# Second feed-forward product of a hybrid layer: from weights standing to tokens standing

## The chip, the cores and the metric

The kernel runs on one core of a Trainium2 chip. The metric is the device time of one execution in microseconds, lower is better. TensorE's matmuls are called PE here and its weight loads PEld; VectorE is DVE, ScalarE ACT, GpSimd POOL, and SP is the engine that issues most transfers.

## The reference, cut to what matters

One layer for 128 context tokens and 512 latent tokens (640 together, 1024 channels): a token mixer, a residual with layer norm, a feed-forward block of width 2816, and a second residual with layer norm. The change is in the last three lines.

```python
x = layer_norm(ALPHA * x + g1 * out, p['ln_gain'][l, 0], p['ln_bias'][l, 0])
h2 = x * (1 + sc2) + sh2
a, u = jnp.split(h2 @ p['w_ffn_in'][l], 2, axis=-1)
f = (jax.nn.silu(a) * u) @ p['w_ffn_out'][l]          # (640, 2816) @ (2816, 1024)
x = layer_norm(ALPHA * x + g2 * f, p['ln_gain'][l, 1], p['ln_bias'][l, 1])
```

`g2` is one vector of 1024 values for the context tokens and another for the latent ones. `layer_norm` goes over the 1024 channels of a token.

## The kernel before, in words

Every large product is made of rounded fp32r parts: an operand is split into a high part and the rest (`w_hi`, `w_lo`; `f_hi`, `f_lo`), and three matmuls (high x high, high x low, low x high) are added up in PSUM. Weights come in units of 128 x 1024 floats (512 KB) by SP's queue into the two slots of `raw`; a unit is split into the two slots of `w_hi` and `w_lo`. Semaphores carry the order: `raw_in` (landed), `w_half` (high part made), `w_split` (both made), `units_done` (PE has used the unit, the slot is free). There is no planner: each engine runs its own program, written out by hand, and SP loads a unit when the one two before it has been split.

**First feed-forward product (L1379 to L1431, L1405 is its matmul).** 22 pairs of 128-channel tiles, by a scheme of seven products per pair. Its results pass through `held`, `quarter_*`, `gate_sum`, `gate_normed`, ACT's `gate`, `unit_sum` and `gated`, the last pair's steps on DVE at L2724 to L2738, and leave in `f_all` (22 tiles of 128 channels x 640 tokens, channels on the partitions). ACT rounds them to `f_hi` (L2022) and DVE makes `f_lo` (`f_rest`, L2688 to L2692, whose subtraction is recorded at L2082). The pairs of weights are loaded by `pair_load` (L712, recorded at L715); the one for the third pair goes out behind the store of the first residual's result to memory (`x1_dram`, L725).

**Second product (L1433 to L1465, matmuls at L987).** Weights stand, tokens move. For each of the 8 tiles of 128 output channels, 22 blocks of weights (three units of 8, 8 and 6 blocks), and for each block three weight parts, each against 640 tokens as a matmul of 256 and one of 384 columns: 132 matmuls a tile, 1056 in all. Two PSUM regions (`joined(0)`, `joined(1)`) take turns, and the first two tiles are interleaved (`FF_ORDER`), because `f_lo` is made while PE already runs (it waits on `f_ok` block by block). POOL makes both halves of every unit (`last_split`: `rounded` at L795, `rest` at L799).

**Residual and rows.** While PE is at the next tile, DVE normalises the stored first-residual result for it (`normed_x1`, L2747), ACT scales it (L2040), DVE adds gate times product to it (`residual`, L2541, recorded at L2546), PE transposes the result, five 128x128 blocks (`to_rows`, L1445, recorded at L1451), ACT copies the rows to `rows2` (L2048) and DVE takes statistics of the 128 columns (`row_stats`, L2757, recorded at L2762).

**End.** After the last channel tile: its residual, transposes, copy, statistics, then `bn_aggr` for the five token tiles (L2779), one square root, one reciprocal (L2797), and for each of four token tiles two 1024-column passes on DVE (`centred` L2785 and `finished` L2791) with gain and bias read from PSUM, while ACT and POOL finish the fifth (L2067, L973, L975). SP stores each token tile when it is finished (L779) and waits for all of them.

**The same form elsewhere.** One earlier product already has tokens standing and 512 weight columns moving: the mixer's `v` projection, L1295 to L1303.

Of the kernel before, what the change touches and what calls it, by code (L numbers as in the profile page):

```python
# [25 lines left out]
F32 = mybir.dt.float32  # L26
F32R = mybir.dt.float32r
# [33 lines left out]
UB = 8  # L61
UW = UB * P
FQ = (UB, UB, KF - 2 * UB)
# [11 lines left out]
U_END = U_FF2 + len(FQ) * KD  # L75
# [4 lines left out]
FF_ORDER = ((0, 0), (1, 0), (0, 1), (1, 1), (0, 2), (1, 2))  # L80
# [43 lines left out]
def build(nc, wunits, wmod1, wmod2, xT, x_fold, cT, c_rows, bmod, consts, dft_pos, dft_x, wnyq, wgate, gate_bias,  # L124
# [3 lines left out]
    with ctx:  # L128
# [8 lines left out]
        x1_dram = nc.dram_tensor("x1_dram", [P, KD, NT], F32, kind="Internal").ap()  # L137

# [216 lines left out]
        assert c2[0] <= t_end  # L355
        x2_all = at("x2_all", [P, KD, NT], F32, c2)
        rows2 = at("rows2", [P, TT, DMODEL], F32, c2)
        ln_row = at("ln_row", [P, 2, DMODEL], F32, c2)
        r2_t = at("r2_t", [P, 2, NT], F32, c2)
        stats2 = at("stats2", [P, TT, KD, 6], F32, c2)  # L360
# [132 lines left out]
        y_ok_p = sem("y_ok_p")  # L493
# [12 lines left out]
        c_read, u_read = Again(bmod_ok, 1), Again(once, 2)  # L506
        pair_in = [Again(mod_in[8], 48), Again(mod_in[9], 48)]

        ln_ps = flat[:, 0:2 * DMODEL].rearrange("p (a c) -> p a c", a=2)
# [46 lines left out]
        def by_half(ap):  # L556

            return ap.rearrange("p (h k) t -> p h k t", h=2)

# [7 lines left out]
        def _(sp):  # L567
# [157 lines left out]
            sp.dma_start(x1_dram, r_all[:]).then_inc(x1_stored, 16)  # L725

# [11 lines left out]
            def unit_load(i, n, p, q, place):  # L738

                w = FQ[q] * P  # L740
                sp.dma_start(place[:, 0:w], wunits[U_FF2 + len(FQ) * (2 * i + p) + q][:, 0:w])\
                    .then_inc(raw_in[n % 2], 16)

            def last_unit(i, n, p, q):

                sp.wait_ge(w_split, C_FF2 + 2 * len(FQ) * i + n - 1)
                unit_load(i, n, p, q, raw[:, n % 2, :])
# [9 lines left out]
            for n in range(2):  # L757
                unit_load(0, n, *FF_ORDER[n], first_raw[:, n * UW:(n + 1) * UW])
            slots_made(KF)
            for n in range(2, 4):  # L760
                sp.wait_ge(w_split, C_FF2 + n - 1)
                unit_load(0, n, *FF_ORDER[n], raw[:, n % 2, :])
# [4 lines left out]
            last_unit(0, 4, *FF_ORDER[4])  # L767
            sp.dma_start(x2_all[:, 2:KD, :], x1_dram[:, 2:KD, :]).then_inc(x_in[1], 16)
            last_unit(0, 5, *FF_ORDER[5])
            sp.wait_ge(f_f_ok, KF)  # L770
            sp.dma_start(ln_row[:], ln_rows).then_inc(table_in, 16)
            with sp.Fori(1, KD // 2) as i:
                for n in range(2 * len(FQ)):
                    last_unit(i, n, n // len(FQ), n % len(FQ))

            for tt in range(TT):
                sp.wait_ge(*((y_ok_p, 2) if tt == TT - 1 else (y_ok, tt + 1)))
                dst = y_prompt if tt == 0 else y_sample[(tt - 1) * P:tt * P, :]
                sp.dma_start(dst, rows2[:, tt, :]).then_inc(y_stored, 16)  # L779
            sp.wait_ge(y_stored, 16 * TT)  # L780
# [4 lines left out]
        def _(pool):  # L785
# [162 lines left out]
            def last_split(i, n, q, src=raw, early=False):  # L948

                slot = n % 2  # L950
                src, hi, lo = (t[:, slot, 0:FQ[q] * P] for t in (src, w_hi, w_lo))
                pool.wait_ge(raw_in[slot], 16 * len(FQ) * i + 16 * (C_FF2 // 2 + n // 2 + 1))
                if not early:
                    pool.wait_ge(units_done, C_FF2 + 2 * len(FQ) * i + n - 1)
                elif slot == 1:
                    pool.wait_ge(prod_done[P7].sem, prod_done[P7].base + KF)
                rounded(src, hi)
                pool.wait_ge(w_half, half1 + 2 * len(FQ) * i + n + 1)
                if early and slot == 1:
# [3 lines left out]
            for n in range(2):  # L963
                last_split(0, n, 0, first_raw.rearrange("p (a c) -> p a c", c=UW), True)
            for n in range(2, len(FF_ORDER)):
                last_split(0, n, FF_ORDER[n][1])
            with pool.Fori(1, KD // 2) as i:
                for n in range(2 * len(FQ)):
                    last_split(i, n, n % len(FQ))

            last = rows2[:, TT - 1, :]
            pool.wait_ge(norm_ok, 2)
            pool.tensor_tensor(last, last, ln_row[:, 0, :], ALU.mult).then_inc(y_ok_p, 1)  # L973
            pool.wait_ge(y_ok_p, 1)
            pool.tensor_tensor(last, last, ln_row[:, 1, :], ALU.add).then_inc(y_ok_p, 1)  # L975
# [3 lines left out]
        def _(pe):  # L979
# [453 lines left out]
            def last_unit(i, n, p, q, ready=None):  # L1433

                if q == 0:
                    pe.wait_ge(taken[p], A_FF2 + i + 1)
                unit_cols(joined(p), C_FF2 + 2 * len(FQ) * i + n, n % 2, f_hi, f_lo, k0=UB * q, nb=FQ[q],
                          first=(q == 0), last=(q == 2), ready=ready)

            def last_tile(i, p):  # L1440

                for q in range(len(FQ)):
                    last_unit(i, len(FQ) * p + q, p, q)

            def to_rows(i, p):  # L1445

                pe.wait_ge(taken[p], A_FF2 + i + 2)
                pe.wait_ge(rows2_ok, 2 * i + p + 1)
                for tt in range(TT):
                    a = (4 + 2 * p) * 512 + tt * P  # L1450
                    ins = pe.transpose(flat[:, a:a + P], r2_t[:, p, tt * P:(tt + 1) * P], ident)  # L1451
                ins.then_inc(rt2_done, 1)

            pe.wait_ge(c_read.sem, c_read.base + KF)
            for n, (p, q) in enumerate(FF_ORDER):
                if n == 1:
                    pe.wait_ge(u_read.sem, u_read.base + KF)
                last_unit(0, n, p, q, f_ok if p == 0 else None)
            to_rows(0, 0)
            with pe.Fori(1, KD // 2) as i:  # L1460
                last_tile(i, 0)
                to_rows(i - 1, 1)
                last_tile(i, 1)
                to_rows(i, 0)
            to_rows(KD // 2 - 1, 1)  # L1465
# [3 lines left out]
        def _(act):  # L1469
# [573 lines left out]
            def row_tile(j, p):  # L2043
# [3 lines left out]
                a = (4 + 2 * p) * 512  # L2047
                A_(dst, flat[:, a:a + NT].rearrange("p (t c) -> p t c", c=P), ACT.Copy).then_inc(rows2_ok, 1)  # L2048

            for j in range(2):  # L2050
                scaled_x1(j)
            row_tile(0, 0)
            with act.Fori(1, KD // 2) as i:
                for p in range(2):
                    scaled_x1(2 * i + p)
                row_tile(2 * i - 1, 1)
                row_tile(2 * i, 0)
            row_tile(KD - 1, 1)
            act.wait_ge(table_in, 64)
            act.wait_ge(taken[0], A_FF2 + KD // 2 + 1)  # L2060
            A_(ln_ps[:, 0, :], ln_row[:, 0, :], ACT.Copy).then_inc(sd_b_ok, 1)
            act.wait_ge(var_b_ok, 2)
            A_(sd[:], sd[:], ACT.Sqrt).then_inc(sd_b_ok, 1)
            act.wait_ge(taken[1], A_FF2 + KD // 2 + 1)
            A_(ln_ps[:, 1, :], ln_row[:, 1, :], ACT.Copy).then_inc(sd_b_ok, 1)
            act.wait_ge(norm_ok, 1)
            A_(rows2[:, TT - 1, :], rows2[:, TT - 1, :], ACT.Identity, scale=rstd[:, TT - 1:TT],  # L2067
               bias=nmr[:, 0:1]).then_inc(norm_ok, 1)
# [3 lines left out]
        def _(v):  # L2072
# [599 lines left out]
            def gated(i):  # L2672

                v.wait_ge(u_read.sem, u_read.base + i + 1)
                v.tensor_tensor(tb[:], tb[:], rstd_ps, ALU.mult).then_inc(tb_ok, 1)
# [50 lines left out]
            sum_7(KF - 1, 1)  # L2726
            f_rest(0, 1)
# [12 lines left out]
            v.wait_ge(w_split, C_FF2 + 3)  # L2740
            f_rest(*range(10, 16))
            v.wait_ge(w_split, C_FF2 + 4)
            f_rest(*range(16, KF))
            v.tensor_copy(rstd_sb[:], rstd_ps).then_inc(rstd_b_ok, 1)
            v.wait_ge(rstd_b_ok, 2)
# [8 lines left out]
            for j in range(2):  # L2754
                normed_x1(j, 0)

            def row_stats(j):  # L2757

                v.wait_ge(rows2_ok, j + 3)
                tiles = rows2[:, :, :].rearrange("p t (j c) -> p t j c", c=P)  # L2760
                for tt in range(TT):
                    ins = v.bn_stats(stats2[:, tt, j, :], tiles[:, tt, j, :])  # L2762
                return ins
# [5 lines left out]
            with v.Fori(1, KD // 2) as i:  # L2769
                for p in range(2):  # L2770
                    normed_x1(2 * i + p, 1)
# [168 lines left out]
```

## Time and profile before

| | |
|---|---|
| median of 3 runs | 1405.27 us (1404.27 to 1405.46) |
| the profiled execution's own time | 1404.05 us |
| its span on the core | 1402.2 us |
| granted TensorE clock, mean | 0.993 of full speed |
| PE / DVE / POOL / ACT busy | 98% / 61% / 57% / 32% of the span |

The profile is one execution; busy time is summed over the span, and PE's matmuls are pipelined, so two of them overlap in the records and only the distance between starts is their real pace. "The chain that ended last" goes back from the last instruction, at each step to what released it. In a row of a timeline the bracket says how long the engine had idled before and what released it.

### The profile page before, as it was taken

What the parts mean: (1) busy time and instruction counts of PE and PEld (TensorE: products, weight loads), DVE (VectorE), ACT (ScalarE), POOL (GpSimd) and SP (SyncE); (2) the same over time, 40 slices, a digit from 0 to 9 for tenths busy, and PEclk for the clock granted to TensorE, in tenths of its full rate; (3) what the DMA queues carried; (4) which work ended last, traced back from release to release, by engine and by line L of the source; (5) the groups of instructions that cost most, each with busy time, mean ns of one, the idle gap of its engine ahead of it and who ended that gap; (6) DMA issues with size and microseconds to landing.
All of it is one profiled execution on the core that took longest, in us unless ns stands there. A gap on an engine that the chain in (4) does not pass through costs nothing. (4 is left out here: it accounts for less than half of the span.)

```text
span 1402.2 us, 24166 instructions
## 1 busy us (share of the span) xinstructions
PE 1369.4 (98%) x9089; PEld 1327.0 (95%) x9089; DVE 862.2 (61%) x1473; ACT 450.3 (32%) x806; POOL 795.5 (57%) x444
## 2 busy tenths in 40 slices
PE   9999999999999999999999999999999999999994
PEld 5999999899999989999999999999999999999994
DVE  6975983357436624752674577587777777892224
ACT  4824221231222122122233100466555445600001
POOL 0264865632552363245235666458998888865662
PEclk9999999999999999999999999999999999999997
DMA  9634633221411321142146454422222221242221
GB/s 379 220 115 139 226 121 132 85 65 50 141 63 68 105 91 60 49 143 74 37 140 230 168 202 156 172 89 109 89 89 90 90 88 63 92 154 84 67 67 75
DMA packets 57483, 164.01 MB, mean 117 GB/s; under 512 B 6072, under 2 KB 20544, under 8 KB 56264
## 3 DMA queue, kind: packets, MB, share of 16 engines
q1 hardware_dynamic: 38712, 142.48, 29.2%
q10 hardware_dynamic: 18704, 20.68, 4.4%
q8 instruction: 36, 0.59, 0.2%
q14 instruction: 31, 0.25, 0.1%
HBM read 145.81 MB, written 17.33 MB: 116 GB/s over the span
## 5 line engine op out<-in xcount | busy, mean ns | idle before, releaser
L795 POOL TENSOR_TENSOR w_hi<-raw,zero 128x1024 fp32r<-128x1024 f32 (+1 forms) x101 | 192.2, 1903 | 436.4 <-PE psum L987 358.6
L799 POOL TENSOR_TENSOR w_lo<-raw,w_hi 128x1024 fp32r<-128x1024 f32 (+2 forms) x116 | 278.7, 2402 | 29.3 <-ACT w_hi L1881 16.9
L1405 PE MATMUL psum<-t_r,ws_r 128*128 128x322 f32 x1848 | 276.6, 311 | 2.0 <-POOL ws_r L871 0.7
L1405 PEld LDWEIGHTS psum<-t_r,ws_r 128*128 128x128 f32 x1848 | 275.1, 189 | 3.2 <-issue 2.0
L987 PE MATMUL psum<-h_hi,w_hi 128*128 128x256 f32 (+1 forms) x768 | 176.4, 311 | 0.3 <-PEq L1341 0.3
L987 PE MATMUL psum<-h_lo,w_hi 128*128 128x256 f32 (+1 forms) x768 | 175.3, 309 | 0.0
L987 PE MATMUL psum<-h_hi,w_lo 128*128 128x256 f32 (+1 forms) x768 | 175.1, 309 | 0.0
L871 POOL TENSOR_TENSOR ws_r<-ws_f,ws_r 128x512 fp32r<-128x512 f32 x88 | 124.4, 1414 | 33.6 <-DVE ws_f L2619 20.8
L987 PEld LDWEIGHTS psum<-h_lo,w_hi 128*128 128x128 f32 x768 | 140.3, 189 | 0.0
L987 PEld LDWEIGHTS psum<-h_hi,w_lo 128*128 128x128 f32 x768 | 140.0, 188 | 0.0
L987 PEld LDWEIGHTS psum<-h_hi,w_hi 128*128 128x128 f32 x768 | 138.7, 189 | 1.4 <-issue 0.7
L871 POOL TENSOR_TENSOR ws_r<-pair,ws_r 128x512 fp32r<-128x512 f32 x66 | 95.7, 1450 | 4.6 <-ACT ws_r L1939 4.6
L987 PE MATMUL psum<-f_hi,w_hi 128*128 128x256 f32 x352 | 81.2, 312 | 1.8 <-DVE f_lo L2082 1.7
L987 PE MATMUL psum<-f_lo,w_hi 128*128 128x256 f32 x352 | 80.1, 309 | 0.0
L987 PE MATMUL psum<-f_hi,w_lo 128*128 128x256 f32 x352 | 80.1, 309 | 0.0
L1939 ACT ACTIVATE ws_r<-ws_f 128x512 fp32r<-128x512 f32 x88 | 54.3, 630 | 71.1 <-POOL ws_f L890 36.8
L987 PEld LDWEIGHTS psum<-f_hi,w_hi 128*128 128x128 f32 x352 | 63.4, 188 | 2.8 <-DVE f_lo L2082 2.5
L2546 DVE SCALAR_TENSOR_TENSOR r_t<-psum,mod_sb,x_all 128x128 f32<-128x128 f32 (+1 forms) x16 | 8.1, 546 | 93.5 <-PE psum L987 93.5
L987 PEld LDWEIGHTS psum<-f_lo,w_hi 128*128 128x128 f32 x352 | 64.1, 188 | 0.0
L987 PEld LDWEIGHTS psum<-f_hi,w_lo 128*128 128x128 f32 x352 | 64.0, 188 | 0.0
L1301 PE MATMUL psum<-w_hi,h_hi 128*128 128x512 f32 x160 | 62.3, 390 | 0.0
L1301 PE MATMUL psum<-w_lo,h_hi 128*128 128x512 f32 x160 | 62.3, 389 | 0.0
(353 smaller groups left out, 3121.9 us busy)
## 6 DMA issues: line engine op xcount, KB each, us to landing
raw<-in_wunits SPq DMA_DIRECT2D x118, 512.0 KB, 3.3
pair<-in_wunits SPq DMA_DIRECT2D x46, 512.0 KB, 4.2
mod_slot<-in_wmod SPq DMA_DIRECT2D x16, 512.0 KB, 14.6
mod_ring<-in_wmod ACTq DMA_DIRECT2D x16, 512.0 KB, 3.4
yg_dram<-yg_sb ACTq DMA_DIRECT2D x20, 256.0 KB, 2.5
yg_st<-yg_dram SPq DMA_DIRECT2D x16, 320.0 KB, 3.6
c_raw<-in_stateC SPq DMA_DIRECT2D x4, 1028.0 KB, 6.2
z_ring<-in_wmod SPq DMA_DIRECT2D x8, 512.0 KB, 4.5
```

Of the source, the lines that this page charges most:

```text
L795: pool.tensor_tensor(hi, src, zero[:, 0:1].broadcast_to([P, src.shape[1]]), ALU.add)\
L799: pool.tensor_tensor(lo, src, hi.bitcast(F32), ALU.subtract).then_inc(w_split, 1)
L871: pool.tensor_tensor(ws_r[n][:, 1, :], src, ws_r[n][:, 0, :].bitcast(F32), ALU.subtract)\
L987: ins = mm(out[:, a:z], w[:, slot, cols], x[:, k, a:z], start=(start and n == 0), stop=(stop and n == 2))
L1301: ins = mm(psum[:, v_banks[tt], :], x[:, k, tt * P:(tt + 1) * P], w[:, q % 2, cols], start=(k == 0 and n == 0), stop=(k == KD - 1 and n == 2))
L1405: ins = mm(out, ws_r[n][:, w, cols], t_r[:, n, k, x, :], start=(starts and k == 0 and m == 0), stop=(k == HALF_K - 1 and m == 2), skip_gro ...
L1939: A_(ws_r[n][:, 0, :], src, ACT.Copy).then_inc(ws_hi_ok[n].sem, 1)
L2546: ins = v.scalar_tensor_tensor(out=out[:, span], in0=src[:, span], scalar=mod_sb[:, gcol + j, g:g + 1], in1=r[:, j, span], op0=ALU.mult, o ...
```

## The change

The second product is turned round. A unit of weights is now two blocks of 128 feed-forward channels (`KU`) times 512 output channels (`UC`); there are 11 units (`NU`) for the left half of the output channels and 11 for the right. A block of `f_hi` or `f_lo` for 128 tokens stands and 512 weight columns move, into one PSUM bank for each token tile: five banks a half (`ROW_BANKS`). So PE issues 2 halves x 11 units x 5 token tiles x 2 blocks x 3 parts = 660 matmuls of 512 columns. In the right half the last four units are kept together (the extra places `last_hi`, `last_lo` hold their parts in memory that has come free) and are run token tile by token tile.

```diff
+            def row_part(h, tt, u, first, last):
+
+                out, toks = psum[:, ROW_BANKS[h][tt], :], slice(tt * P, (tt + 1) * P)
+                hi, lo = unit_slot(u)
+                for n in range(KU):
+                    k, cols = KU * (u % NU) + n, slice(n * UC, (n + 1) * UC)
+                    if h == 0 and tt == 0:
+                        pe.wait_ge(f_ok, k + 2)
+                    for m, (f, w) in enumerate(((f_hi, hi), (f_hi, lo), (f_lo, hi))):
+                        ins = mm(out, f[:, k, toks], w[:, cols], start=(first and n == 0 and m == 0),
+                                 stop=(last and n == KU - 1 and m == 2))
+                return ins
...
+            BANK_FREE = ((u_read.sem, u_read.base + KF - 1), (c_read.sem, c_read.base + KF),
+                         (c_read.sem, c_read.base + KF), (ta_ok, KF), (u_read.sem, u_read.base + KF))
+            for u in range(NU):
+                pe.wait_ge(w_split, C_FF2 + SPLITS.index(u) + 1)
...
+                if 2 <= u < KD + 2:
+                    x1_to_rows(u - 2)
+            pe.wait_ge(rows2_ok, KD + 2)
+            for u in range(NU, FIRST_LAST):
...
+                    if u == NU and tt >= 3:
+                        pe.wait_ge(row_sum_ok, tt - 2)
...
+            for tt in range(TT):
+                for u in range(FIRST_LAST, 2 * NU):
...
+                ins.then_inc(tile_done, 1)
```

The first-residual result alone (not the sum) is transposed, tile by tile between the left half's units 2 to 9 (`x1_to_rows`); ACT copies it to `rows2`. When a half of a token tile is complete, DVE multiplies the bank by `g2` and adds it to `rows2` (`row_sum`). `g2` must for this lie along the columns: SP writes it from `mod_sb` (channels on partitions) to memory in two transfers, right behind the store of the first-residual result and ahead of the third pair's weights, and reads it back to all partitions later.

```diff
             sp.dma_start(x1_dram, r_all[:]).then_inc(x1_stored, 16)
+            sp.wait_ge(mod_sum1, 5 * KD)
+            for g in range(2):
+                sp.dma_start(g2_dram[g].rearrange("k p -> p k"), mod_sb[:, 5 * KD:6 * KD, g],
+                             allow_slow_non_contiguous=True).then_inc(g2_stored.sem, 16)
...
+            sp.dma_start(g2_row[:], g2_dram.rearrange("g k p -> g (k p)").unsqueeze(0).broadcast_to([P, 2, DMODEL]))\
+                .then_inc(g2_in.sem, 16)
```

From the third unit on, ACT makes the high part (`unit_hi`) and POOL only the rest. On DVE the last pair's `unit_sum` and `gated` move ahead of most of `f_rest`, and the copy of the first norm's reciprocal from PSUM (L2744) moves ahead of all of it; `normed_x1` and two `f_rest` each then alternate, held back by `w_split`.

```diff
             sum_7(KF - 1, 1)
+            v.tensor_copy(rstd_sb[:], rstd_ps).then_inc(rstd_b_ok, 1)
+            v.wait_ge(rstd_b_ok, 2)
             f_rest(0, 1)
...
-            f_rest(*range(3, 7))
+            f_rest(3)
             unit_sum(KF - 1, 1)
-            f_rest(7)
-            gated(KF - 1)
-            f_rest(8, 9)
...
+            gated(KF - 1, rstd_sb[:])
+            f_rest(4, 5)
...
+            for j in range(KD):
+                v.wait_ge(w_split, C_FF2 + j + 3)
+                normed_x1(j, 0 if j < 2 else 1)
+                f_rest(2 * j + 6, 2 * j + 7)
...
+            def row_sum(h, tt):
+
+                n, ps, g = TT * h + tt, psum[:, ROW_BANKS[h][tt], :], min(tt, 1)
+                cols = slice(h * UC, (h + 1) * UC)
+                v.wait_ge(tile_done, n + 1)
+                v.tensor_tensor(ps, ps, g2_row[:, g, cols], ALU.mult).then_inc(scaled_ok.sem, 1)
+                v.wait_ge(scaled_ok.sem, scaled_ok.base + n + 1)
+                v.tensor_tensor(rows2[:, tt, cols], ps, rows2[:, tt, cols], ALU.add).then_inc(row_sum_ok, 1)
+                v.wait_ge(row_sum_ok, n + 1)
+                return v.bn_stats(stats2[:, tt, h, :], rows2[:, tt, cols])
...
             for tt in range(TT):
+                row_sum(0, tt)
+            for tt in range(TT):
+                own(row_sum(1, tt))
+                own(v.bn_aggr(mv[:, tt, :], stats2[:, tt, :, :]))
+                v.tensor_scalar(sd[:, tt:tt + 1], mv[:, tt, 1:2], EPS, None, ALU.add).then_inc(var_b_ok, 1)
...
+                parts = [slice(0, DMODEL)] if tt < TT - 1 else [slice(0, UC), slice(UC, DMODEL)]
+                for n, cols in enumerate(parts):
+                    centred(tt, cols, tt + n)
+                v.wait_ge(sd_b_ok, tt + 2)
+                own(v.reciprocal(rstd[:, tt:tt + 1], sd[:, tt:tt + 1]))
+                for n, cols in enumerate(parts):
+                    finished(tt, cols, tt + n)
```

ACT takes the square root of one token tile at a time; gain and bias are read from `ln_row` in SBUF; all five token tiles are finished by DVE, and the last one is finished and stored in two halves of its columns. The host lays the weights of `w_ffn_out` out in the new units.

## Rows read from the trace of the kernel before

**Rows 1.** the page: span, and busy time by engine

```profile
span 1402.2 us, 24166 instructions
...
PE 1369.4 (98%) x9089; PEld 1327.0 (95%) x9089; DVE 862.2 (61%) x1473; ACT 450.3 (32%) x806; POOL 795.5 (57%) x444
```

**Rows 2.** chain that ended last, from 1215 us: start, us, what

```profile
1282.92 0.55 PE psum L1451 x5
...
1363.18 19.39 PE psum L987 x132
```

**Rows 3.** timeline of PE, 1215 to 1262 us: start, us, engine, line, out<-in

```profile
1221.49 0.56 PE L987 MATMUL psum<-f_hi,w_hi 128*128 128x256 f32 x2
...
1243.37 0.56 PE L987 MATMUL psum<-f_hi,w_hi 128*128 128x256 f32 x2 [0.96 <-DVE f_lo L2082]
```

**Rows 4.** timeline of PE, 246 to 260 us, tokens standing: first and last of 58 matmuls

```profile
246.68 0.39 PE L1301 MATMUL psum<-w_hi,h_hi 128*128 128x512 f32 x1
...
259.62 0.39 PE L1301 MATMUL psum<-w_hi,h_hi 128*128 128x512 f32 x1
```

**Rows 5.** timeline of DVE, 1205 to 1290 us

```profile
1222.21 4.70 DVE L2082 TENSOR_TENSOR f_lo<-f_all,f_hi 128x640 fp32r<-128x640 f32 x4
...
1227.02 1.13 DVE L2668 SCALAR_TENSOR_TENSOR tb<-nmu,w,psum 128x128 f32<-128x128 f32 x3
```

**Rows 6.** weight halves: POOL's timeline, then the instructions of L1881

```profile
1279.70 2.39 POOL L799 TENSOR_TENSOR w_lo<-raw,w_hi 128x1024 fp32r<-128x1024 f32 x1
...
L1881 ACT ACTIVATE w_hi<-raw x6: 1041/1046/1062, 890.6 to 927.8; 128x1024 fp32r<-128x1024 f32 x6
```

**Rows 7.** a 128x512 sum on DVE, timeline

```profile
1040.68 0.69 DVE L2619 TENSOR_TENSOR ws_f<-ws_f,pair 128x512 f32<-128x512 f32 x1
```

**Rows 8.** timeline of all engines, 1382 to 1402.2 us

```profile
1382.72 1.01 DVE L2546 SCALAR_TENSOR_TENSOR r_t<-psum,mod_sb,x_all 128x128 f32<-128x128 f32 x2 [17.44 <-PE psum L987]
...
1384.12 2.27 DVE L2762 BATCH_NORM_STATS2 stats<-rows  x10 [0.39 <-ACT rows L2048]
...
1386.43 1.29 DVE L2779 BATCH_NORM_AGGREGATE mv<-stats 128x2 f32<-128x48 f32 x5
...
1387.83 1.27 DVE L2785 SCALAR_TENSOR_TENSOR rows<-rows,mv,psum 128x1024 f32<-128x1024 f32 x1
...
1389.02 0.18 DVE L2797 RECIPROCAL rstd<-sd 128x5 f32<-128x5 f32 x1
...
1394.19 4.40 SPq L779 DMA_DIRECT2D out_y_sample<-rows  x4
...
1395.27 2.47 DVE L2791 SCALAR_TENSOR_TENSOR rows<-rows,rstd,psum 128x1024 f32<-128x1024 f32 x2
```

**Rows 9.** waits of SP's queue: total us, times, longest

```profile
SPq L128 <- DMA out_y_sample<-rows: 3.2, 1, 3.2
```

**Rows 10.** SP's timeline; a window: DMA share and GB/s; DMA issues (page)

```profile
952.38 51.48 SPq L715 DMA_DIRECT2D pair<-in_wunits  x10
...
950.00:951.00 1.00, 1.00 0.34 143
...
pair<-in_wunits SPq DMA_DIRECT2D x46, 512.0 KB, 4.2
```

**Rows 11.** timelines of ACT and POOL, then the chain, around 960 us

```profile
960.67 0.62 ACT L1939 ACTIVATE ws_r<-pair 128x512 fp32r<-128x512 f32 x1
...
965.40 1.29 POOL L871 TENSOR_TENSOR ws_r<-ws_f,ws_r 128x512 fp32r<-128x512 f32 x1
...
958.68 258.48 PE psum L1405 x1736
```

**Rows 12.** queues: of the whole span (page), then 39 to 46 us: packets, MB, share

```profile
q10 hardware_dynamic: 18704, 20.68, 4.4%
...
DMA packets 967, 2.62 MB, mean 374 GB/s; under 512 B 558, under 2 KB 558, under 8 KB 965
...
q1 hardware_dynamic: 965, 2.60, 101.3%
```

More of the change, by code:

```diff
@@ L756, in _ @@
             slots_made(KF - 1)
-            for n in range(2):
-                unit_load(0, n, *FF_ORDER[n], first_raw[:, n * UW:(n + 1) * UW])
+            for m in range(2):
+                unit_load(m, first_raw[:, m * UW:(m + 1) * UW])
             slots_made(KF)
-            for n in range(2, 4):
-                sp.wait_ge(w_split, C_FF2 + n - 1)
-                unit_load(0, n, *FF_ORDER[n], raw[:, n % 2, :])
+            unit_load(2)
             sp.wait_ge(prod_done[P4].sem, prod_done[P4].base + KF)
@@ L946, in _ @@
             half1 = half0 + U_FF1 - U_HEAD
[L948 to L959, printed above, removed]
+            for m in range(2 * NU):
+                src = first_raw[:, m * UW:(m + 1) * UW] if m < 2 else raw[:, m % 2, :]
+                hi, lo = unit_slot(SPLITS[m])
+                if m < 2:
+                    pool.wait_ge(raw_in[m], 16 * (C_FF2 // 2 + 1))
+                    if m == 1:
+                        pool.wait_ge(prod_done[P7].sem, prod_done[P7].base + KF)
+                    rounded(src, hi)
+                pool.wait_ge(w_half, half1 + m + 1)
+                if m == 1:
                     pool.wait_ge(prod_done[P4].sem, prod_done[P4].base + KF)
                 rest(src, hi, lo)
[L963 to L975, printed above, removed]
         @block.tensor
@@ L1431, in _ @@
             product(P4, KF - 1, 1)
[L1433 to L1448, printed above, removed]
+            def row_part(h, tt, u, first, last):
[9 more added lines that the diff above has]
+                return ins
@@ new lines, in _ @@
+            pe.wait_ge(rows2_ok, KD + 2)
+            for u in range(NU, FIRST_LAST):
+                pe.wait_ge(w_split, C_FF2 + SPLITS.index(u) + 1)
+                for tt in range(TT):
+                    if u == NU and tt >= 3:
+                        pe.wait_ge(row_sum_ok, tt - 2)
+                    ins = row_part(1, tt, u, u == NU, False)
+                ins.then_inc(units_done, 1)
+            for tt in range(TT):
+                for u in range(FIRST_LAST, 2 * NU):
+                    if tt == 0:
+                        pe.wait_ge(w_split, C_FF2 + SPLITS.index(u) + 1)
+                    ins = row_part(1, tt, u, False, u == 2 * NU - 1)
+                ins.then_inc(tile_done, 1)
@@ L2041, in scaled_x1, with row_tile @@
                    bias=ln_cols[:, j, 1:2]).then_inc(x1_ok, 1)
[L2043 removed]
+            def row_tile(j):
                 act.wait_ge(rt2_done, j + 1)
                 dst = rows2[:, :, :].rearrange("p t (j c) -> p t j c", c=P)[:, :, j, :]
[L2047 to L2052 removed]
@@ L2053, in _ @@
[L2053 to L2068, printed above, removed]
+                A_(dst, strip(1).rearrange("p (t c) -> p t c", c=P), ACT.Copy).then_inc(rows2_ok, 1)
+            def unit_hi(m):
+                u = SPLITS[m]
+                act.wait_ge(raw_in[m % 2], 16 * (C_FF2 // 2 + m // 2 + 1))
+                if m == 2:
+                    act.wait_ge(w_split, C_FF2 + 2)
+                if u == FIRST_LAST:
+                    act.wait_ge(rt2_done, KD)
+                elif FIRST_LAST < u < 2 * NU - 1:
+                    act.wait_ge(units_done, C_FF2 + NU + 1)
+                elif u == 2 * NU - 1:
+                    act.wait_ge(units_done, C_FF2 + FIRST_LAST - 2)
+                elif u == NU + 1:
+                    act.wait_ge(tile_done, TT)
+                else:
+                    act.wait_ge(units_done, C_FF2 + u - 1 - (u > NU + 1))
+                A_(unit_slot(u)[0], raw[:, m % 2, :], ACT.Copy).then_inc(w_half, 1)
@@ L2071, in _ @@
+            for m in range(2, 4):
+                unit_hi(m)
+            for j in range(KD):
+                scaled_x1(j)
+                unit_hi(4 + j)
+                row_tile(j)
+            for m in range(KD + 4, 2 * NU):
+                unit_hi(m)
+            for tt in range(TT):
+                act.wait_ge(var_b_ok, tt + 2)
+                A_(sd[:, tt:tt + 1], sd[:, tt:tt + 1], ACT.Sqrt).then_inc(sd_b_ok, 1)
         @block.vector
@@ L2752, in normed_x1 @@
                 v.tensor_tensor(x2_all[:, j, :], x2_all[:, j, :], rstd_sb[:], ALU.mult).then_inc(t2_ok, 1)
[L2754 to L2763, printed above, removed]
-            for p in range(2):
-                v.wait_ge(x1_ok, p + 1)
-                residual(p, p, C_FF2 + FF_ORDER.index((p, len(FQ) - 1)) + 1, x2_all, 5 * KD, r2_t[:, p, :])
@@ L2768, in _ @@
-            row_stats(0)
-            with v.Fori(1, KD // 2) as i:
-                for p in range(2):
-                    normed_x1(2 * i + p, 1)
-                v.wait_ge(x1_ok, 2 * i + 2)
-                for p in range(2):
-                    v.wait_ge(rt2_done, 2 * i + p - 1)
-                    residual(2 * i + p, p, C_FF2 + 2 * len(FQ) * i + len(FQ) * (p + 1), x2_all, 5 * KD, r2_t[:, p, :])
-                    row_stats(2 * i + p - 1)
-            own(row_stats(KD - 1))
-            for tt in range(TT):
-                ins = v.bn_aggr(mv[:, tt, :], stats2[:, tt, :, :])
@@ L2794, in _ @@
-            v.wait_ge(sd_b_ok, 2)
-            centred(0)
-            v.wait_ge(sd_b_ok, 3)
-            own(v.reciprocal(rstd[:], sd[:]))
-            v.scalar_tensor_tensor(out=nmr[:, 0:1], in0=mv[:, TT - 1, 0:1], scalar=-1.0, in1=rstd[:, TT - 1:TT],
-                                   op0=ALU.mult, op1=ALU.mult).then_inc(norm_ok, 1)
-            centred(1)
-            v.wait_ge(sd_b_ok, 4)
-            finished(0)
-            for tt in range(2, TT - 1):
-                centred(tt)
-                finished(tt - 1)
```

137 lines of the change are left out of this document (78 added, 59 removed).

## The prediction, made blind

> **What bounds the kernel now.** I read the page first: PE is busy 98% of a span of 1402.2 us [rows 1]. Then the chain of waits from 1215 us on: it is PE's own matmuls, channel tile after channel tile, 132 matmuls of the second product in 19.39 us and then five transposes in 0.55 us [rows 2]. No other engine holds PE up there, so what counts is PE's pace in that stage, its few stalls at the start, and everything that comes after its last matmul. The stage runs from 1221.49 [rows 3] to 1363.18 + 19.39 = 1382.57 [rows 2], 161.1 us; after it come 19.6 us of epilogue in which PE does next to nothing. The change works on both.
>
> **Pace of PE.** Before: 132 matmuls are 66 pairs of 256 and 384 columns, so 19.39/66 = 0.2938 us per 640 columns. Eight tiles are 155.1 us. After: 660 matmuls of 512 columns. The kernel already has this very form, tokens standing and 512 weight columns moving; its 58 matmuls start from 246.68 to 259.62, 12.94/57 = 0.2270 us apart [rows 4]. 660 x 0.2270 = 149.8 us. The columns are the same (337,920); what goes is a cost per matmul, about 13 ns, 396 times. Gain 5.3 us.
>
> The Trainium skill, in TensorE: Matmul & The Clock Gate, section Back-to-back issue gap, gives the warm distance of two lone matmuls as columns/2.4 + 2.5 ns. By that rule a pair would take 271.7 ns and a 512 matmul 215.8, and the turn would bring 1.0 us, not 5.3. Both of this trace's distances are longer, the shorter form by more.
>
> **Stalls and transposes.** 8 x 19.39 + 7 x 0.55 = 159.0, so 161.1 holds 2.1 us of stalls: PE waits for `f_lo` three times, the longest 0.96 us before 1243.37 [rows 3]. They come from the first tile needing 22 blocks of `f_lo` in about 22 us. After, the first unit needs two blocks and keeps PE for 30 x 0.227 = 6.8 us, so 22 blocks are spread over 75 us; those stalls go. All eight transposes now lie within the stage (before, the eighth was in the epilogue): 8 x 0.55 = 4.4 us.
>
> What could be late next? **Banks:** the fifth token tile of the first unit wants the bank that `unit_sum` reads, at 1221.49 + 4 x 1.36 = 1226.9. That step is at 1227.02 now, behind four `f_rest` of 4.70/4 = 1.18 us from 1222.21 [rows 5]. With one `f_rest` ahead of it, it is over by 1222.2 + 1.2 + 1.3 = 1224.7: 2 us to spare. The moved copy of the reciprocal adds about 0.8 us to DVE earlier; nothing but these steps stands behind it, and twice it would still fit. **Weights:** a unit's slot comes free when the unit two before it is done; ACT's high part takes 1.05 us, POOL's rest 2.39 [rows 6], together 3.5 us of the 6.8 that PE spends on the unit between. Loads fit in the same way. **`f_rest`:** each step of DVE's loop is two of them and two 640-column passes, some 4 us, twice a unit ahead. The turned order thus costs PE nothing; the cover is 3 us everywhere, and if it went, each unit would cost what is missing.
>
> PE's last matmul then ends at 1221.49 + 149.8 + 4.4 + 0.16 (its record is 0.39 long, its distance 0.23 [rows 4]) = 1375.9, 6.7 us earlier.
>
> **Epilogue.** Before: 1382.57 to 1402.2, of which DVE's passes over all rows last until 1395.27 + 2.47 = 1397.74 [rows 8]. After, each token tile ends 24 x 0.227 = 5.45 us behind the one before it, and DVE deals with four of them under PE. Per tile, from rows: product and sum in PSUM, 512 columns each, 0.69 [rows 7] plus 0.04 for the semaphore, so 1.46; statistics of 512 columns: no row, at least the 0.2 us of a 128-column one, at most another 512-column pass; I take 0.69, since the columns set the time of the other passes; aggregate 1.29/5 = 0.26; root's input 0.08; the two 1024-column passes 1.19 each (1387.83 to 1389.02); reciprocal 0.22 [rows 8]. Sum 5.1 us, under 5.45: no queue builds up. ACT's root lies under the first pass. For the last tile, in halves: 0.15 to start (1382.57 to 1382.72), 1.46, 0.69, 0.26, 0.08, 1.22, 0.22, 1.30 = 5.4 us. Then the stores: before, DVE's end to the span's end is 4.46 us, of which the last of four queued stores is issued until 1394.19 + 4.40 = 1398.59 [rows 8] and SP waits 3.2 us for it [rows 9]. After, the last half row is issued at once: 0.1 + 0.35 + 3.2 + 0.4 = 4.05. The smaller store may land sooner or, with rows of 2 KB, later: -0.7 to +0.7.
>
> New end: 1375.9 + 5.4 + 4.05 = 1385.3 against 1402.2: **16.9 us**, 6.7 from PE's stage and 10.2 from the epilogue. The profiled execution took 1404.05, which gives 1387.2; the median of the runs lies 1.2 above that execution, so I say **1388.4**.
>
> **The new transfers of `g2`.** They are the one thing that the trace does not price: 2 x 1024 values of 4 bytes, each with an address of its own, 128 for each of 16 DMA engines, behind the store that ends near 951 (the window from 950 still shows 0.34) and ahead of the third pair's weights, issued at 952.38 and landed 4.2 us later [rows 10]. Nearest rows: queue q10 over the span, 0.044 x 1402.2 x 16/18704 = 53 ns a packet; q1 from 39 to 46 us, where 558 of 967 packets are under 512 bytes: 1.013 x 7 x 16/965 = 118 ns a packet [rows 12]. So 128 packets are 6.8 to 15 us, and the weights land at 951 + 6.8 + 4.2 = 962.0 to 970.2. Who waits? ACT uses them at 960.67, and POOL's rest for P1 of the third pair is in order ahead of the one for P7 of the second, which starts at 965.40 [rows 11]. Counting back from 1221.49 at 258.48/1736 = 0.149 us a matmul [rows 11], 1692 matmuls, P1 starts at 969.5 and that P7 at 967.7; its slot is ready at 966.7, so there is 1 us to spare, and the weights may land until about 964.5. I take 53 ns (such packets carry next to nothing, and the second row's carry 2.7 KB on average): no cost. At 118 ns PE stalls 5.7 us. Reading `g2` and `ln_row` back is 1 MB each in a stage with DMA mostly idle: nothing.
>
> **Rivals.**
> - *Forecast holds:* 0.70.
> - *The small packets are dear, but not very (73 to 205 ns):* PE stalls 5.7 us at 118 ns, so 1394.1. For it: no row has such writes to memory. Against: loads of small packets pass among others at 118 ns at most. 0.11.
> - *Slower than before:* the same mechanism from 205 ns a packet on, where 128 packets take 26.2 us, the landing moves to 981.4 and PE's stall to 16.9 us; at 300 ns the stall is 29 us and the time 1417. 0.04. The Trainium skill, in DMA: Bandwidth & Descriptors, says under Rules for kernel authors that a strided last dimension becomes a descriptor per element, and under Specifications that below 512 bytes there is read-modify-write; it gives no price, and no row here shows one.
> - *DVE falls behind:* the tiles are then not normalised as they end. If a tile takes over 5.45 us (it would need 0.35 more, for example by passes on SBUF operands at the 1.27 us record rather than the 1.19 distance, and slower statistics), four excesses add up: at 6.4 us a tile, 4 us, so 1392. 0.05.
> - *PE waits in the new order* (a split or a bank late at the start or where the halves meet): 3 to 5 us, 1392. Against: 3 us of cover each time. 0.06.
> - *Nothing is saved per matmul:* the new form keeps the old one's time per column here, 0.2938 x 512/640 = 0.2350 us, and only stalls and epilogue gain: 1393.7. Against it stands the pace of [rows 4]. 0.04. By the rule of the Trainium skill cited above it would be 1392.7.
>
> **How the numbers follow.** Forecast's own spread is about -2.5 to +2 (statistics, last store, stalls that hide others). To hold 8 in 10 the range reaches to the sizes of the milder rivals: 1385.5 to 1394. A difference of 0.2%, 2.8 us, is about what a measurement of this kernel can tell from none. All cases but the dear packets are faster by far more: faster 0.94; around 200 ns a packet, same 0.02; beyond, slower 0.04.
>
> **What would show it.** Right: 660 matmuls 0.227 us apart from 1221.5 on, and no PE idle over 0.3 us until about 1376; the five last tile groups 5.45 us apart, DVE idle some 0.3 us between them; DVE's last pass 5.4 us behind the last matmul, the span's end 4 us on. The third pair's weights landed before 964.5 and the first product still ending at 1221.5. Wrong: ACT, DVE or POOL waiting for `pair` near 960 and PE idle near 968 (packets); `w_split` or DVE's `f_lo` releasing PE within the stage; DVE without idle time at the end and its last pass more than 7 us behind PE; 512-column matmuls at another distance than 0.227.

## The result, and the profile after

The changed kernel takes 1388.8 us in the median of 4 runs (1387.98 to 1391.49) against 1405.4 us before; the ratio is 0.9888, with a 95% interval from 0.9877 to 0.9900. The forecast was 1388.4. The profiled execution took 1387.98 us, its span is 1385.9.

The page's first rows, answering to [rows 1]:

```profile
span 1385.9 us, 23137 instructions
...
PE 1361.4 (98%) x8693; PEld 1293.3 (93%) x8693; DVE 854.0 (62%) x1458; ACT 466.1 (34%) x827; POOL 748.6 (54%) x418
```

The chain of waits of the changed kernel, from 940 and from 1215 us on (start, us, what), answering to [rows 2]:

```profile
951.53 12.99 DMA pair<-in_wunits
...
1223.70 20.45 PE psum L1455 x90
1244.14 0.55 PE psum L1465 x5
1244.69 6.86 PE psum L1455 x30
...
1296.39 81.63 PE psum L1455 x360
```

The last four rows are the new second product: 90 matmuls in 20.45 us and 360 in 81.63 are 0.227 us each, with no stall between, and the transposes are the same 0.55 us as before. The stage runs from its first matmul at 1223.54 to DVE's start on the last tile at 1378.04, 154.5 us, where it was 161.1. The first row is not of that stage. The chain of before has no transfer near that place; here it waits 13 us for the third pair's weights.

The timeline of DVE in the epilogue, the fourth token tile and the last one, answering to [rows 8]:

```profile
1372.61 0.70 DVE L2800 TENSOR_TENSOR psum<-psum,g_row 128x512 f32<-128x512 f32 x1 [0.27 <-PE psum L1455]
1373.34 0.69 DVE L2802 TENSOR_TENSOR rows<-psum,rows 128x512 f32<-128x512 f32 x1
1374.06 0.69 DVE L2804 BATCH_NORM_STATS2 stats<-rows 128x6 f32<-128x512 f32 x1
1374.79 0.21 DVE L2823 BATCH_NORM_AGGREGATE mv<-stats 128x2 f32<-128x12 f32 x1
...
1376.49 1.28 DVE L2814 SCALAR_TENSOR_TENSOR rows<-rows,rstd,ln_row 128x1024 f32<-128x1024 f32 x1
1378.04 0.70 DVE L2800 TENSOR_TENSOR psum<-psum,g_row 128x512 f32<-128x512 f32 x1 [0.27 <-PE psum L1455]
...
1382.06 1.42 DVE L2814 SCALAR_TENSOR_TENSOR rows<-rows,rstd,ln_row 128x512 f32<-128x512 f32 x2
```

Read the brackets: DVE idles 0.27 us before each of these two tiles, so it is ready when PE is, and each tile takes it 1378.04 - 0.27 - 1372.61 = 5.16 us out of PE's 5.43. The last one takes 1383.48 - 1378.04 = 5.44. The stores then end sooner than before, by SP's waits (total us, times, longest), answering to [rows 9]:

```profile
SPq L134 <- DMA out_y_sample<-rows: 1.6, 1, 1.6
```

From DVE's end to the span's end it is 2.4 us; it was 4.46. The whole epilogue is 7.9 us, it was 19.6.

What was lost is at the start of the first feed-forward product. The timeline of PE there, and the two rows of ACT's that release it:

```profile
957.74 6.71 PE L1418 MATMUL psum<-t_r,ws_r 128*128 128x322 f32 x44
965.55 2.05 PE L1418 MATMUL psum<-t_r,ws_r 128*128 128x322 f32 x12 [1.10 <-ACT held L1981]
969.76 6.49 PE L1418 MATMUL psum<-t_r,ws_r 128*128 128x322 f32 x41 [2.16 <-ACT held L1981]
...
964.54 0.63 ACT L1971 ACTIVATE ws_r<-pair 128x512 fp32r<-128x512 f32 x1 [5.36 <-DMA pair<-in_wunits]
...
969.29 0.42 ACT L1981 ACTIVATE held<-psum 128x322 f32<-128x322 f32 x1
```

ACT used the third pair at 960.67 without waiting [rows 11]; now it idles 5.36 us for it, and PE waits 3.3 us for `held`, which stands behind on ACT.

The balance of the two profiled executions: PE's stage -6.6 us, epilogue -11.7, and from the first product's first matmul to the second product's first +3.6 (280.6 to 284.2 us). The stages ahead, which the change does not touch, were 1.6 us shorter in this execution; over the traces of this study the first product starts anywhere between 939.1 and 942.3 us, so that part is drift. Together that is -16.3, the difference of the spans.

### The profile page after: what moved, and what is told of

It is laid out like the page before. It is cut to its first block and busy times, and to the rows that moved or that the text cites. A ratio compares the mean times of both kernels' runs of the same rounds, so it can differ in the third digit from the quotient of the medians.

```text
span 1385.9 us, 23137 instructions
## 1 busy us (share of the span) xinstructions
PE 1361.4 (98%) x8693; PEld 1293.3 (93%) x8693; DVE 854.0 (62%) x1458; ACT 466.1 (34%) x827; POOL 748.6 (54%) x418
## 5 line engine op out<-in xcount | busy, mean ns | idle before, releaser
L824 POOL TENSOR_TENSOR w_hi<-raw,zero 128x1024 fp32r<-128x1024 f32 x79 | 152.2, 1926 | 376.4 <-PE psum L1000 298.1
L828 POOL TENSOR_TENSOR w_lo<-raw,w_hi 128x1024 fp32r<-128x1024 f32 (+1 forms) x111 | 269.8, 2431 | 101.1 <-ACT w_hi L2097 73.5
L1455 PE MATMUL psum<-w_hi,f_hi 128*128 128x512 f32 x190 | 74.7, 393 | 0.0
L1455 PE MATMUL psum<-w_hi,f_lo 128*128 128x512 f32 x190 | 74.1, 390 | 0.0
L1455 PE MATMUL psum<-w_lo,f_hi 128*128 128x512 f32 x190 | 73.9, 389 | 0.0
L1314 PE MATMUL psum<-w_hi,h_lo 128*128 128x512 f32 x160 | 62.2, 389 | 0.0
L1000 PE MATMUL psum<-yh,w_hi 128*128 128x256 f32 (+1 forms) x256 | 58.6, 311 | 0.0
L1000 PE MATMUL psum<-yh,w_lo 128*128 128x256 f32 (+1 forms) x256 | 58.3, 308 | 0.0
L1000 PE MATMUL psum<-yl,w_hi 128*128 128x256 f32 (+1 forms) x256 | 58.1, 308 | 0.0
```

The lines of the kernel that those rows point to most:

```text
L824: pool.tensor_tensor(hi, src, zero[:, 0:1].broadcast_to([P, src.shape[1]]), ALU.add)\
L828: pool.tensor_tensor(lo, src, hi.bitcast(F32), ALU.subtract).then_inc(w_split, 1)
L1000: ins = mm(out[:, a:z], w[:, slot, cols], x[:, k, a:z], start=(start and n == 0), stop=(stop and n == 2))
L1314: ins = mm(psum[:, v_banks[tt], :], x[:, k, tt * P:(tt + 1) * P], w[:, q % 2, cols], start=(k == 0 and n == 0), stop=(k == KD - 1 and n == 2))
L1455: ins = mm(out, f[:, k, toks], w[:, cols], start=(first and n == 0 and m == 0), stop=(last and n == KU - 1 and m == 2))
```

## The experiments

The runs form three groups, each on one chip, and each kernel is compared with the kernel before on its chip. The first group holds the changed kernel, the stores moved, the stores doubled and the 256-column matmuls; the second holds the stores on ACT's queue and the two runs with fewer units kept; the third holds the rest. The second group has no run of the changed kernel, so what it says is read from its traces more than from its times. For the start of the first product one length is used: from its first matmul (940.91 in the kernel before) to the second product's first matmul (1221.49).

**The changed kernel twice more**, as the base of the first and of the third group.

> The changed kernel once more, as the base that the other runs of this call are set against. Expected by all theories: 1388 to 1391 us, the second product's PE stage 154.3 us long, about 2 us of PE waits for ACT's held rows early in the first feed-forward product.

Measured: 1393.4 us (1392.5 to 1394.9), ratio 0.9930, interval 0.9914 to 0.9947. That is 4.6 us above the first result, above what was expected here and near the upper edge of the prediction's range (1394).

> The changed kernel a third time, with more rounds, for the interval: 1388 to 1394.

Measured: 1389.1 us (1388.0 to 1390.0), ratio 0.9887 (0.9871 to 0.9904). The second product's stage and the epilogue are the same in all three, 154.5 and 7.9 us. The length at the start is not: 284.2, 286.9 and 284.8 us, where it was 280.6 before. The windows of PE show part of why (busy us and instructions, granted clock, DMA share, GB/s); first the execution of the result, then the one of 1393 us:

```profile
965.00:970.00 5.00, 2.29 (x13) 1.00 0.00 0
970.00:975.00 5.00, 5.00 (x34) 1.00 0.60 205
```

```profile
965.00:970.00 5.00, 2.65 (x18) 1.00 0.45 171
970.00:975.00 5.00, 3.71 (x16) 0.54 0.00 0
975.00:980.00 5.00, 5.00 (x28) 0.78 0.61 210
```

PE sits idle for 3.3 us in the one and 3.6 in the other, but in the second its granted clock then falls to the lower of its two levels for some microseconds, for (0.46 + 0.22) x 5 = 3.4 us at full speed. Part of that falls into the time in which PE idles anyway: the start is 6.3 us longer than before, so 6.3 - 3.6 = 2.7 us are lost beside the idle time. In the first execution the clock stays at 1.00.

**The stores of `g2` moved behind the last pair.**

```diff
             sp.dma_start(x1_dram, r_all[:]).then_inc(x1_stored, 16)
-            sp.wait_ge(mod_sum1, 5 * KD)
-            for g in range(2):
-                sp.dma_start(g2_dram[g].rearrange("k p -> p k"), ...
...
             for i in range(2, KF):
                 pair_next(i, i % 2)
+            sp.wait_ge(mod_sum1, 5 * KD)
+            for g in range(2):
+                sp.dma_start(g2_dram[g].rearrange("k p -> p k"), ...
```

> The two stores of g2 go out behind the last pair of weights instead of ahead of the third. Theory A (the 4-byte packets delay the third pair, and PE pays): PE's waits at the start of the first product go, the third pair lands some 4 us after its issue, the time falls by 3.6 us against the changed kernel, to about 1385.2. Theory B (the late start of the second product is another execution's drift and not the packets): no change, 1388 to 1389. If the packets were as harmful in the new place, the first two units of the second product would land late (after 1214) and the time would not fall.

> The version with the stores behind the last pair again, with more rounds: 1385 to 1387, 3.6 to 7 us below the changed kernel.

Measured: 1386.1 us (1384.6 to 1387.1) beside 1393.4, and 1385.8 us (1384.1 to 1388.8) beside 1389.1; ratios to the kernel before 0.9876 (0.9860 to 0.9893) and 0.9869 (0.9850 to 0.9888). That is 7.3 and 3.3 us less than the changed kernel of the same group, where 3.6 and 3.6 to 7 were expected. The length at the start is 280.3 us both times, PE has no wait for `held`, the clock stays at 1.00, and ACT uses the third pair, issued at 952.62, without waiting:

```profile
960.91 0.62 ACT L1971 ACTIVATE ws_r<-pair 128x512 fp32r<-128x512 f32 x1
```

Theory A holds, B falls. The two units loaded behind the stores in the new place land in time: POOL rounds the first at 1215.48 without waiting for it (1214.73 in the kernel before). They are issued from 1203.10 on, 11.6 us behind the stores, so this run does not show that the stores are harmless there to a load issued at once. This version is the fastest of the study, though in the third group its interval overlaps the changed kernel's.

**The stores made twice.**

```diff
             for g in range(2):
                 sp.dma_start(g2_dram[g].rearrange("k p -> p k"), mod_sb[:, 5 * KD:6 * KD, g],
                              allow_slow_non_contiguous=True).then_inc(g2_stored.sem, 16)
+            for g in range(2):
+                sp.dma_start(g2_dram2[g].rearrange("k p -> p k"), mod_sb[:, 5 * KD:6 * KD, g],
+                             allow_slow_non_contiguous=True).then_inc(g2_stored.sem, 16)
```

> The two stores of g2 are made twice in the same place, the second time to another place in memory, 4096 packets in all. Theory A, with the packets at the 80 ns each per DMA engine that the trace of the changed kernel suggests (about 10 us for 2048): the third pair lands 10 us later than in the changed kernel, all of it stalls PE, 1399 us. Theory A with a fixed cost for a DMA rather than one for a packet: the same here, since the DMAs double too. Theory B: 1389. If what counts is not the ring's order, PE stalls by much less than 10 us.

Measured: 1398.7 us (1398.0 to 1400.4), ratio 0.9966. The length at the start is 295.1 us, 14.8 more than without stores in this place; ACT idles 16.20 us for the pair:

```profile
947.80 7.83 SPq L754 DMA_DIRECT2D g_dram<-mod_sb  x2
956.22 5.60 SPq L738 DMA_DIRECT2D pair<-in_wunits  x2
...
976.97 0.63 ACT L1975 ACTIVATE ws_r<-pair 128x512 fp32r<-128x512 f32 x1 [16.20 <-DMA pair<-in_wunits]
```

So the cost grows about as A has it: the length at the start is 8 to 11 us above that of the three executions with two stores. PE idles 12.6 us of it, and the clock is at its lower level from 971 to 981. Part of it is new: SP itself was held up, and issued the pair at 956.2 instead of about 952.5.

**One store instead of two** (the context tokens' gate is left out and the latent tokens' used for both).

```diff
-            for g in range(2):
+            for g in range(1, 2):
                 sp.dma_start(g2_dram[g].rearrange("k p -> p k"), mod_sb[:, 5 * KD:6 * KD, g],
```

> Only the latent tokens' g2 is stored, 1024 packets instead of 2048, and read back for the context tokens too (their gate is left out). Theory G (the time goes with the packets, some 80 to 100 ns each per DMA engine, 10 to 12 us for 2048): the third pair lands 5 to 6 us earlier than in the changed kernel and PE's waits for ACT's held rows go: as fast as with the late stores, 1385 to 1387. Rival H (a fixed completion time of about 10 us for writes of this kind): the pair lands as late as in the changed kernel, and the 3.6 to 6.3 us of stall stay.

Measured: 1389.1 us (1387.6 to 1389.9), the time of the changed kernel in the same group. The length at the start is 284.6 us. The pair is used 12.4 us after its issue at 951.21; with both stores it was 12.5 to 14.7:

```profile
963.65 0.64 ACT L1971 ACTIVATE ws_r<-pair 128x512 fp32r<-128x512 f32 x1 [4.38 <-DMA pair<-in_wunits]
```

Theory G falls: half the packets, nearly the same delay. Rival H is nearer for one store against two, but alone it does not explain the four of the run before. How the cost depends on the count of packets and of transfers, and whether it lies in the single elements written to memory or in how they are gathered, stays open: no run stored the same values in longer pieces.

**The stores from ACT's queue.** The same lines, moved ahead of ACT's wait for the column sums.

> The two stores of g2 go out from ACT's queue, ahead of its wait for the column sums, at about the same moment as in the changed kernel. Theory E (the weights waited for their turn behind the packets in one ring): the third pair lands within 5 us of its issue, PE loses at most what ACT's own delay costs (2 x 1.4 us of issue, of which about 1.5 us were idle), 1385 to 1387. Theory F (the packets keep the DMA engines or memory busy whichever ring they are in): the pair lands as late as in the changed kernel, 1389 or more.

Measured: 1391.4 us (1388.6 to 1393.1), ratio 0.9912 (0.9895 to 0.9930). The pair is issued at 950.59 and used at 965.14, 14.5 us later, though its ring held no packet of the stores. The length at the start is 285.0 us. Theory E falls and F holds: it is not the order in the ring. The windows of that execution (granted clock, DMA share, GB/s) show hardly any data on the way:

```profile
951.00:952.00 1.00, 1.00 0.00 0
952.00:953.00 1.00, 1.00 0.00 0
953.00:954.00 1.00, 1.00 0.00 0
...
959.00:960.00 1.00, 1.00 0.20 20
...
962.00:963.00 1.00, 1.00 1.01 328
```

The DMA engines are silent for three microseconds, trickle at some 30 GB/s for eight, and only then move the pair at over 300. In this run the stores have a queue of their own, so their packets can be counted apart (packets, MB, share of 16 engines, 948 to 966 us):

```profile
q10 hardware_dynamic: 2080, 0.01, 5.3%
```

That is 0.053 x 18 x 16/2080 = 7 ns a packet, and all of them have gone by 951. Their own time is thus even less than the prediction took; what costs is the silence and the trickle behind them. In the result's execution the two stores land 16.1 and 17.5 us after their issue, near 959 and 960, just before the pair's data comes at full rate; which of the two causes the other these rows do not show.

**ACT's order in the second pair's cycle.**

```diff
                 hold(0, i, par)
-                slot_hi(P1, i + 1, 1 - par)
+                if not pending:
+                    slot_hi(P1, i + 1, 1 - par)
                 hold(1, i, par)
                 slot_hi(P7, i, par)
+                if pending:
+                    slot_hi(P1, i + 1, 1 - par)
```

> Stores of g2 in their place, but in ACT's first cycle the high part of the third pair's P1 comes behind hold(1) and P7's high part instead of ahead of them. Theory J (PE waits because hold(1) stands behind the late pair on ACT, which the prediction's deadline of 964.5 left out): PE's wait for held rows goes (3.3 to 3.6 us); what remains is POOL's rest for P7, which still stands behind P1's, up to 3 us when the pair lands at 968. Time 0.5 to 3 us below the changed kernel's of the same call. Rival: no change, since POOL's order alone sets the stall.

Measured: 1388.4 us (1387.8 to 1389.9) beside 1389.1: nothing that can be told from no change. One of PE's two waits for `held` is gone, the other is 2.45 us. Theory J named the right engine and the wrong one of its instructions. The length at the start is 284.6 us. The chain of waits of this run:

```profile
964.41 0.70 DVE ws_f L2656
...
965.79 1.28 ACT L1988
...
967.46 0.61 ACT psum L1989
968.06 0.55 ACT ws_r L1971
968.62 0.33 ACT held L1981
...
968.99 6.13 PE psum L1418 x29
```

DVE's sum for P5 needs the late pair, ACT's high part needs the sum, and behind it on ACT stand a table load of 1.28 us (its row bears the gate's line), the first gate, P4's high part, and then `hold(2)`, for which PE waits. POOL, on which the prediction had its deadline, is not on this chain.

**Two matmuls of 256 columns for each of 512.**

```diff
-                        ins = mm(out, f[:, k, toks], w[:, cols], start=(first and n == 0 and m == 0),
-                                 stop=(last and n == KU - 1 and m == 2))
+                        for a in range(0, UC, UC // 2):
+                            b = slice(a, a + UC // 2)
+                            ins = mm(out[:, b], f[:, k, toks], w[:, cols][:, b],
+                                     start=(first and n == 0 and m == 0 and a == 0),
+                                     stop=(last and n == KU - 1 and m == 2), skip_group_check=True)
```

> Each 512-column matmul of the second product is cut into two of 256, with the same block standing: 1320 matmuls. Theory C (a cost of 13 to 14 ns per matmul, whatever its columns): the pair takes 0.2407 us instead of 0.2270, the stage grows by 9.0 us to 163.3, 1397.8 us in all. By the rule of columns/2.4 + 2.5 ns for each: growth 1.6 us, 1390.4. If the cost hangs on the change of the standing block rather than on the matmul: 1388.8, no growth.

Measured: 1400.8 us (1397.4 to 1403.4), beside 1393.4 for the base; the start costs more in this execution too (287.4 us), so the stage is what counts. It runs from 1229.74 to DVE's start at 1392.59, 162.8 us instead of 154.5: 8.35 us for 660 matmuls more, 12.7 ns each. The chain of waits of this run ends with

```profile
1349.96 42.61 PE psum L1457 x355
...
1392.59 0.71 DVE psum L2803
```

which is 0.120 us a matmul. Theory C holds nearly at its size; the other two fall. The weight loads grew with the matmuls, though (9353 of each, where it was 8693): the same block is loaded again for the second half. So a cost for each matmul cannot be told here from a cost for each load.

**Fewer units kept for the last tiles.** `N_LAST` is the count of units run token tile by token tile at the end.

```diff
-N_LAST = 4
+N_LAST = 1
...
-SPLITS = (*range(NU + 2), FIRST_LAST, NU + 2, ...
+SPLITS = tuple(range(2 * NU))
```

> Only the right half's very last unit is run with its tiles ending one by one (6 matmuls, 1.36 us apart) instead of the last four (24 matmuls, 5.45 us apart). Theory D (DVE's 5.17 us a tile, measured in the changed kernel, sets the epilogue where PE is faster): DVE starts 5.45 us ahead of PE's end and needs 4 x 5.17 + 5.4 + 0.1, the epilogue grows from 7.9 to about 23 us, the time by 15.2 us to 1404. Rival: the gain of the epilogue comes from the shorter DVE work and the missing transposes, not from the overlap: growth under 5 us.

Measured: 1405.4 us (1403.1 to 1408.0), ratio 1.0009 (0.9999 to 1.0018). PE's last matmul ends at 1381.6, and DVE goes on (its timeline, one row a tile):

```profile
1376.19 0.70 DVE L2791 TENSOR_TENSOR psum<-psum,g_row 128x512 f32<-128x512 f32 x1 [64.33 <-PE psum L1452]
...
1381.28 0.69 DVE L2791 TENSOR_TENSOR psum<-psum,g_row 128x512 f32<-128x512 f32 x1
...
1396.52 0.69 DVE L2791 TENSOR_TENSOR psum<-psum,g_row 128x512 f32<-128x512 f32 x1
```

A tile each 5.08 us, no idle time, and an epilogue of 1404.4 - 1381.6 = 22.8 us, 14.9 more than with four units. Theory D said 15.2.

> The last two units are run tile by tile (12 matmuls, 2.72 us apart). Theory D: the first tile is ready 10.9 us ahead of PE's end, growth 20.7 - 10.9 = 9.8 us, 1398.6. Rival as in the run before: growth under 3 us.

Measured: 1404.4 us (1400.9 to 1406.9), more than expected. The epilogue is 17.2 us (PE ends at 1384.5, the span at 1401.7), 9.3 more than with four units, where D said 9.8. The rest is a stall that no theory had: the second of the two last units is wanted after six matmuls, 1.4 us, and its slot comes free too late for ACT and POOL to fill it; PE waits 2.3 us for `w_lo`, and its clock then falls to the lower level (0.66 of full speed from 1370 to 1375), 0.34 x 5 = 1.7 us more. The whole stage is 158.5 us instead of 154.5. In the changed kernel, with its extra places for the weights, PE has no such wait.

## Why the prediction was right, and where it was not

It came out within 0.4 us of the median, but not because each term was right, and that it came so near is luck. In spans, 16.9 us less were forecast and 16.3 measured: a missed cost of 3.6 us stands against a missed gain of 1.5 in the epilogue and 1.6 of drift in stages that the change does not touch. The same kernel, run again, came out at 1393.4 and 1389.1.

- **Pace of PE, gain 5.3 us: right.** 0.227 us a matmul throughout the stage, and the cut into 256 columns gives the cost per matmul, its weight load with it, as 12.7 ns where I took 13. The Trainium skill (TensorE: Matmul & The Clock Gate, Back-to-back issue gap) has 2.5 ns, for lone matmuls; by that the cut would have cost 1.6 us, and it cost 8.35. So the figure does not hold for this stream, in which each matmul has a weight load of its own.
- **Stalls, gain 2.1, and one more set of transposes: right.** Stage predicted 154.4, measured 154.5. Banks, weights and `f_rest` cost PE nothing.
- **Epilogue, DVE: right.** 5.1 us a tile and 5.4 for the last against 5.16 and 5.44. The statistics of 512 columns, for which there was no row, took the 0.69 us of another pass. That the tiles end one by one is worth 15 us: with one unit kept the kernel gained nothing against the kernel before, 4.3 us of `g2`'s stall included (284.9 us at the start).
- **Epilogue, stores: too dear by 1.6 us.** I carried over SP's wait of 3.2 us, in which the last store stood behind three others. Alone and half as large it took 1.6; which of the two counts was not tried.
- **Stores of `g2`, no cost: wrong.** This is the step that failed: "I take 53 ns (such packets carry next to nothing...): no cost". Both parts of it were off. The size: it had the pair landed at 962.0, 9.6 us after its issue at 952.38, and the pair was used 13.4 us after its issue. The form, so much a packet, was wrong too: the packets took some 7 ns each, and one store delays nearly as much as two. The deadline: I took 964.5 from POOL's order. The true one is on ACT, by these rows of the kernel before:

```profile
963.05 0.64 ACT L1939 ACTIVATE ws_r<-ws_f 128x512 fp32r<-128x512 f32 x1 [0.91 <-DVE ws_f L2612]
963.70 1.28 ACT L1956 ACT_TABLE_LOAD   x1
...
966.44 0.42 ACT L1949 ACTIVATE held<-psum 128x322 f32<-128x322 f32 x1
```

The last is `hold(2)` of the second pair. It is over at 966.86, and PE wants it at 958.68 + 60 x 0.149 = 967.6, so 0.7 us are to spare there. From the pair's use to the table load ACT takes 3.03 us here and 2.01 when the pair is late, 1.0 more. So the pair had to be there by about 960.67 + 1.7 = 962.4, an estimate. Each error counts: 962.0 would have met even this deadline, and landing at 952.38 + 13.4 = 965.8 misses it by 3.4 us, against 1.3 by the one that I took. The late pair was ahead of a high part, a table load and a gate in ACT's program, and I had asked only what stood behind it on POOL. Cost: 3.6 to 6.3 us in the three executions of the changed kernel, in part through the clock after the stall. The prediction's own sign for this, ACT waiting for `pair` near 960 and PE idle near 968, is what the trace shows. The rival "dear, but not very" had it at 0.11 and 5.7 us.
- **The rival on the slow side** looks like the run with the stores doubled: a start 14.8 us longer took back most of the gain (ratio 0.9966).

## What to carry to other kernels

Turning a product so that fewer, longer matmuls do the same columns pays by the matmuls saved times some 13 ns here, and the larger part may lie behind it: with results ending tile by tile, normalising goes under PE, as long as the tiles are spaced wider than DVE's time for one. A transposing store of single elements belongs where no transfer is awaited soon, on whatever queue. For a load that a new transfer can delay, follow the waiting instruction on every engine that uses it to what stands behind it in program order, table loads included.

## What the runs showed of the hardware that was not expected

- Two stores of 4 KB each in 4-byte elements kept the DMA engines from moving a 1 MB load for 8 to 10.5 us beyond its usual 4, on the other queue as well (14.5 us against 4.2), though the stores' own packets took 7 ns each and were gone by 951. What the DMA share shows meanwhile differs: between 0.00 and 0.5 from 951 to 960 in the execution of the result, 0.82 (at 37 GB/s) from 955 to 960 with one store, 1.09 (at 1 GB/s) there with four, where the packets took 30 ns each. One such store does it nearly as well as two; two more add 8 to 11 us and hold SP's issue up by 3.7. DMA: Bandwidth & Descriptors in the Trainium skill names a read-modify-write below 512 bytes (Specifications); whether that is what takes the time, no run here shows.
- A short stall can cost TensorE's clock as well, and its length alone does not decide it. PE had been busy for some 7 us before the first stall of each execution. After 2.2 us idle in the run with one store, 2.2 and 0.2 in the third execution of the changed kernel, and 2.3 and 1.3 in the second, the granted clock went from its upper level (2.4 GHz) to its lower one (1.2 GHz) for some microseconds (0.54 to 0.88 of full speed over 5 us). After 1.1 and 2.2 us in the first execution, and 1.9 and 2.2 with the stores from ACT's queue, it stayed at 1.00. The loss beside the idle time was 1.8 us in the third execution and 2.7 in the second.
